# Two halves of 256 tokens: the second half's attention and routing placed between the row gathers of the first

## What is computed

```python
# attention: 8 MLA heads and 8 "fox" heads, causal, on h = modulate(rmsnorm(x)); x = x + gate * (o @ w_o)
# then, with h = modulate(rmsnorm(x)):
qp = (h @ w_pq).reshape(b, s, 8, 2, 128)
sc = einsum("bshpd,hpnd->bshpn", qp, sub_keys)           # 2 x 128 scores for each token and head
s1, i1 = top_k(sc[..., 0, :], 16); s2, i2 = top_k(sc[..., 1, :], 16)
top_s, top_c = top_k(s1[..., :, None] + s2[..., None, :], 16)
expert = i1[top_c // 16] * 128 + i2[top_c % 16]           # one of 16384
g = softmax(top_s)
a = einsum("bcd,bchkd->bchk", h, peer_u[expert])          # one row of 1024 floats for each choice
y = einsum("bchk,bchkd->bcd", g * gelu(a), peer_v[expert])
```

## Time and profile before

| | |
|---|---|
| profiled execution | 3415.21 us, span 3413.4 us |
| first block and final norm | 0 to 1295 us |
| attention of the second block, 512 tokens | 1295 to 1834 us |
| norm and routing up to the first gather | 1834 to 1891 us |
| gathers, dots and sums | 1891 to 3413 us |
| PE, DVE, ACT, POOL busy over the span | 80%, 56%, 29%, 48% |
| DMA | 666.49 MB; software queue (gathers) 41.6% of 16 engines' time, hardware queue 12.5% |

### The profile page before, as it was taken

The page is one execution under the profiler, slowest core; times in us unless marked ns, Lnnn a source line. Parts: engine busy times, 40 slices in busy tenths (PEclk is TensorE's granted clock), DMA queues, the critical chain, the costliest instruction groups (busy, mean ns, idle before and its releaser), DMA issues. The chain is left out here.

```text
span 3413.4 us, 37062 instructions
## 1 busy us (share of the span) xinstructions
PE 2742.4 (80%) x12788; PEld 1837.1 (54%) x12788; DVE 1909.3 (56%) x3608; ACT 1002.9 (29%) x1912; POOL 1623.8 (48%) x1464
## 2 busy tenths in 40 slices
PE   6997879999999697687988888777776777767777
PEld 6997878888889693244655333223222322222323
DVE  5366556666666754665443655555555555555552
ACT  2222155555555211322332122212212212222211
POOL 2443265555555230110001566666666666666665
PEclk8998989998989798888999999998988889989899
DMA  3333411111111341001102799999999999999998
GB/s 97 96 88 124 151 50 50 49 49 49 49 47 39 97 150 37 27 0 37 38 19 80 286 370 328 364 377 356 361 375 357 357 369 363 359 361 365 359 369 310
DMA packets 343486, 666.49 MB, mean 195 GB/s; under 512 B 22181, under 2 KB 209738, under 8 KB 343098
## 3 DMA queue, kind: packets, MB, share of 16 engines
q0 software_dynamic: 147456, 536.94, 41.6%
q1 hardware_dynamic: 194906, 127.75, 12.5%
q10 hardware_dynamic: 992, 0.13, 0.0%
HBM read 662.64 MB, written 2.10 MB: 195 GB/s over the span
## 5 line engine op out<-in xcount | busy, mean ns | idle before, releaser
L1867 PE MATMUL peer_py<-peer_vb,peer_diag 128*128 128x512 f32 x2048 | 1036.9, 655 | 353.1 <-issue 177.5
L1867 PEld LDWEIGHTS peer_py<-peer_vb,peer_diag 128*128 128x128 f32 x2048 | 405.5, 208 | 959.4 <-issue 767.9
L1716 DVE SCALAR_TENSOR_TENSOR peer_spare<-peer_ub,peer_hp 128x1024 bf16<-128x1024 f32 x512 | 623.5, 1218 | 475.9 <-DMA peer_ub<-in_peer_u,peer_idx 416.0
L1611 POOL DMA_INDIRECT peer_vb<-in_peer_v,peer_idx x512 | 480.3, 938 | 351.9 <-issue 140.9
L1603 POOL DMA_INDIRECT peer_ub<-in_peer_u,peer_idx x512 | 483.6, 945 | 169.7 <-issue 137.6
L1800 ACT ACTIVATE peer_diag<-keep_ident,peer_wt 128x128 f32<-128x128 f32 x512 | 190.8, 397 | 994.5 <-PE peer_py L1867 388.8
L862 PE MATMUL hgrn_pp<-p2n_hh,hgrn_wh 128*128 128x264 f32 x1024 | 226.4, 304 | 27.6 <-POOL hgrn_wl L733 27.6
L733 POOL TENSOR_TENSOR hgrn_wl<-p2n_w,hgrn_wh 128x1024 fp32r<-128x1024 f32 x64 | 153.9, 2405 | 180.4 <-ACT hgrn_wh L770 180.4
L862 PE MATMUL hgrn_pp<-p2n_hl,hgrn_wh 128*128 128x264 f32 x1024 | 218.1, 296 | 0.0
L862 PE MATMUL hgrn_pp<-p2n_hh,hgrn_wl 128*128 128x264 f32 x1024 | 216.7, 294 | 0.0
L862 PEld LDWEIGHTS hgrn_pp<-p2n_hh,hgrn_wh 128*128 128x128 f32 x1024 | 171.0, 203 | 28.9 <-POOL hgrn_wl L733 28.4
(11 more groups left out here) (369 smaller groups left out, 4762.7 us busy)
## 6 DMA issues: line engine op xcount, KB each, us to landing
p2n_w<-in_hgrn_w_in SPq DMA_DIRECT2D x64, 512.0 KB
p1n_w<-in_pool_w_in SPq DMA_DIRECT2D x32, 512.0 KB
pool_out_aw<-in_w_ada SPq DMA_DIRECT2D x16, 768.0 KB, 4.7
hgrn_out_aw<-in_w_ada SPq DMA_DIRECT2D x16, 768.0 KB, 4.9
pool_out_w<-in_pool_w_out SPq DMA_DIRECT2D x8, 1024.0 KB, 7.2
hgrn_out_w<-in_hgrn_w_out SPq DMA_DIRECT2D x8, 1024.0 KB, 6.7
p_w<-in_w_pq SPq DMA_DIRECT2D x8, 1024.0 KB
peer_ub<-in_peer_u,peer_idx POOLq DMA_INDIRECT x512
```

Source lines behind the costliest of these rows:

```text
L1611: pool.indirect_dma_start(out=vb[:, n % DEPTH, :], out_offset=None, in_=io["peer_v_2"], in_offset=bass.IndirectOffsetOnAxis(ap=idx[:, s, k ...
L1716: dve.scalar_tensor_tensor(out=spare[:, n % 2, :], in0=ub[:, n % DEPTH, :], scalar=1.0, in1=hp[:, t % 2, :], op0=ALU.mult, op1=ALU.mult, a ...
L1867: last = pe.matmul(py[:, h * 512:(h + 1) * 512], diag[:, n % DIAGS, :], vb[:, n % DEPTH, h * 512:(h + 1) * 512], start=n % (PH * TOPK) == ...
```

## The change

The second block is done for tokens 0 to 255 first, and then for tokens 256 to 511. All its phases take `half` and work on W = 256 columns. The keys and values of the first half are kept (`k_mla`, `k_fox`, `v_mla`, `v_fox`) for the second. `product_phase` is replaced for the attention's output by plain fp32 products (`attn_out_phase`). All weights of the second block are loaded twice.

`peer_phase` becomes a class `Peers` of 532 numbered ticks. At tick T GpSimd issues the u gather of step T + 6 and the v gather of step T - 15, VectorE does the dot of step T, ScalarE the diagonal and TensorE the sum of step T - 20. `beat(n)` runs n ticks at a place in another phase's lists, the same number on each of the four engines. 75 ticks lie in the routing of the first half (15 beats of 5), 8 in the norm, 21 in `latent_phase`, 60 in MLA, 60 in fox, 16 in the output product and 8 in the norm of the second half, 75 in its routing, and the last 209 in `finish_phase`. The h operand of the dot is copied from PSUM to `ht` in SBUF. `pr` of the heads has two banks in place of three, `pT_` one in place of two, and the fox weights of the second half one buffer.

```diff
+def norm_phase(nc, name, x, out, gain, tokens, shift=None, halves=None, ahead=None, beat=None):
...
+        def walk(entries, unit, name):
             for slot in range(U):
                 entries(0, slot)
+                beat(name)
             for g in range(N * U):
                 unit(g, lambda: entries(g // U + 1, g % U) if g // U + 1 < N else None)
+                beat(name)
...
+            slots = [[("raw", 0), ("raw", 2), ("raw", 1), ("raw", 3)],
+                     [("ones", r) for r in order] + [("v", 0), ("rot", 0)],
+                     [("rot", 2), ("rot", 1)], [("rot", 3)]]
...
+UNITS = TT * PH
+SLOTS = UNITS * TOPK
+U_BUFS, V_BUFS, DIAGS = 6, 6, 4
+U_LEAD, V_LAG, Y_LAG = 6, 15, 20
+TICKS = SLOTS + Y_LAG
+class Peers:
...
+        if tick + U_LEAD < SLOTS:
+            gather_u(tick + U_LEAD)
+        if 0 <= tick - V_LAG < SLOTS:
+            gather_v(tick - V_LAG)
...
+            dve.wait_ge(self.u_in[tick % U_BUFS], 16 * (tick // U_BUFS + 1))
+            if tick >= 2:
+                dve.wait_ge(self.dotted, tick - 1)
+            dve.scalar_tensor_tensor(out=self.spare[:, tick % 2, :], in0=self.ub[:, tick % U_BUFS, :], scalar=1.0,
+                                     in1=self.ht[:, t % HT, :], op0=ALU.mult, op1=ALU.mult,
+                                     accum_out=self.a[:, s, k:k + 1]).then_inc(self.dotted, 1)
...
+            pe.wait_ge(self.v_in[n % V_BUFS], 16 * (n // V_BUFS + 1))
+            pe.wait_ge(self.diag_done, n + 1)
...
         def _(pool):
+            for r in range(R):
                 pool.wait_ge(hit_in, r + 1)
                 which = bf[:, r % 2].rearrange("p j (a k) -> p j a k", k=1).to_broadcast([P, 2, TOPK, TOPK])
                 pool.tensor_tensor(hit[:, r % 2], hit[:, r % 2], which, ALU.mult).then_inc(hit_out, 1)
+                if r >= 1:
+                    peers.known = first + r
+                    beat("pool")
...
+            for r in range(R):
+                if r + 2 < PH:
+                    project(r + 2)
+                if r + 2 < R:
+                    scores(r + 2)
+                if r >= 1:
+                    beat("pe")
...
+            with Phase(nc, "hm0") as phh:
+                attention(0, phh.sb("hm", [P, KC, W]), lambda ticks: no_beat)
+            clear_semaphores(nc)
+            with Phase(nc, "peer") as ph4:
+                peers = Peers(nc, io, keep, ph4, out)
+                routing(0, peers, lambda ticks: no_beat)
+                peers.level()
+                attention(1, xT[:, :, 0:W], peers.beat)
+                peers.level()
+                routing(1, peers, peers.beat)
+                peers.level()
+                finish_phase(nc, peers)
```

More of the change, by code:

```diff
@@ L1399, in unit @@
                 values(g - 1)
-            walk(entries, unit)
+            walk(entries, unit, "pe")
             values(N * U - 1)
@@ new lines, in finish_phase, with _, load_queries @@
+def finish_phase(nc, peers):
+    with Phase(nc, "finish") as ph:
+        blk = ph.block()
+        @blk.tensor
+        def _(pe):
+            peers.run("pe", TICKS)
+        @blk.scalar
+        def _(act):
+            peers.run("act", TICKS)
+        @blk.vector
+        def _(dve):
+            peers.run("dve", TICKS)
+        @blk.gpsimd
+        def _(pool):
+            peers.run("pool", TICKS)
+def load_queries(io, sp, w, w_in, n):
+    view = io["w_pq_2"].rearrange("(k p) n -> p k n", p=P)
+    sp.dma_start(w[:, n % 2], view[:, :, n * 2 * P:(n + 1) * 2 * P]).then_inc(w_in[n % 2], 16)
@@ L1540, in peer_phase, with route_phase @@
+def route_phase(nc, io, keep, h2, w, w_in, peers, half, beat):
+    R = HT * PH
+    first = half * R
+    with Phase(nc, f"route{half}") as ph:
         skT = ph.sb("skT", [P, PH, 2, P])
-        qT = ph.sb("qT", [P, PH, 2, SEQ])
+        qT = ph.sb("qT", [P, PH, 2, W])
+        sc = ph.sb("sc", [P, 3, 2, NK])
         best = ph.sb("best", [P, 2, TOPK])
@@ L1582, in _ @@
                 sp.wait_ge(projected, 2 * (n - 1))
-                load(sp, n, n % 2)
-            for t in range(TT):
-                sp.wait_ge(y_taken, t + 1)
-                sp.dma_start(out[0, t * P:(t + 1) * P, :], rows[:, t % 2, :]).then_inc(stored[t % 2], 16)
-            for b in range(2):
-                sp.wait_ge(stored[b], 16 * TT // 2)
+                load_queries(io, sp, w, w_in, n)
         @blk.gpsimd
         def _(pool):
-            def chosen(r):
+            for r in range(R):
                 pool.wait_ge(hit_in, r + 1)
@@ L1807, in _ @@
+                if r >= 1:
+                    peers.known = first + r
+                    beat("pool")
+            peers.known = first + R
         @blk.tensor
@@ L1840, in scores @@
                 last.then_inc(scored, 1)
-            project(0, 0)
-            project(0, 1)
+            project(0)
             scores(0)
+            project(1)
+            scores(1)
             turn_h(0)
-            for n in range(1, 4):
-                project(n, 0)
-                project(n, 1)
-                scores(n)
-            for c in range(KC):
-                last = pe.matmul(py[:, c * P:(c + 1) * P], mod[:, 5 * KC + c:5 * KC + c + 1].to_broadcast([P, P]),
-                                 ident[:, :], start=True, stop=True)
@@ new lines, in routing, with route_ahead @@
+            def routing(half, peers, beat):
+                x = xT[:, :, half * W:(half + 1) * W]
+                with Phase(nc, f"p4{half}") as ph4:
+                    w = ph4.sb("w", [P, 2, KC, 2 * P])
+                    w_in = [ph4.sem("w_in0"), ph4.sem("w_in1")]
+                    def route_ahead(sp):
+                        for n in range(2):
+                            load_queries(io, sp, w, w_in, n)
+                    norm_phase(nc, f"mod2{half}", x, oT, col("norm2_g_2"), W,
+                               lambda c: mod[:, 3 * KC + c:3 * KC + c + 1], ahead=route_ahead, beat=beat(4))
+                    route_phase(nc, io, keep, oT, w, w_in, peers, half, peers.beat(5))
```

870 lines of the change are left out of this document (470 added, 400 removed).

## The result

The changed kernel takes 3510.8 us (median of 4 runs, 3499.1 to 3514.3) where the kernel before takes 3409.9 (4 runs, 3402.6 to 3417.6): ratio 1.0293, 95% interval 1.0266 to 1.032. It is 3% slower. I had forecast 3370, which would have been faster; 3511 lies at the upper edge of the stated range (3245 to 3515), on the side that I had given 0.29.

A forecast was written before the change was run, and what follows sets the result against it. Gather stage bound by DMA transfers, with 596 us ahead of it in which they could run. First gather 1636 + 245 + 647 + 268 + 581 = 3377 span, 3379 executed, lowered by 9 to 3370; own range 3300 to 3440, stated 3245 to 3515.

The forecast's parts named there:

- Part 1: Second block's first half alone, up to the first gather: 341 us in place of 596, first gather at 1636.
- Part 2: Price of one tick: DMA 2.88 us, POOL 2.97 including 0.49 for gathers held by dots reading two SBUF operands.
- A: Routing of half 0 with 75 ticks in 15 beats of 5: 245 us.
- B: Attention of half 1 with its norms, 173 ticks: 647 us, where pure transfer would be 498.
- Part 3: The woven stage from the first gather on: A 245, B 647, C 268, D 581 us.
- MLA: PE 9.6 a beat, POOL 10.1: Half 1's MLA in B, us per beat on each engine: 230 us with the start.
- R3: Rival, lockstep: each unit's chain is paid behind its ticks, B 800 us, total 3530; chance 0.13.
- C: Routing of half 1 with 75 ticks: 25 for its start plus 15 beats of 16.2, 268 us.
- Norm and latent: In B, half 1: 29 ticks, 84 us for DMA plus 9 for weights plus tail, 98 us.
- the last norm with the start of C: Norm 27 us; C's start 25, with rows under way covering some 12 of PE's projections and turns.
- Late weights: Sign that the forecast would be wrong: the weights' loads waiting behind the gathers.
- D: Last 209 ticks, 387 gathers at 1.45 us plus 20 for the tail: 581 us.

The follow-up runs named there:

- run 14: Changed kernel with u gather lead 3 for 6 in most of B, first weights loaded a block earlier, dot reading h from PSUM in A, C, D: 3413.6 us, ratio 1.0039.
- run 18: Kernel of run 15 again, on a 3305 chip: 3320.1 us.
- Run 4: Changed kernel with two ticks in place of three beside every unit of MLA and fox, 3305 chip: 3474.9 us.
- run 9: Changed kernel with u lead 3 and v lag 17 only beside norm, latent, MLA and output product of half 1, 3305 chip: 3396.8 us.
- run 10: Changed kernel with the attention's squares moved from POOL to ScalarE and its cosine products to DVE, 3305 chip: 3419.6 us.
- run 1: Changed kernel with half 1's attention and norms run without ticks, B's 173 ticks in a stage of their own, 3305 chip: 3523.8 us.
- run 13: Kernel of run 9 with half 1's first weights of MLA, fox and output product loaded one block earlier, 3405 chip: 3421.8 us.
- run 16: Kernel of run 15 with PE also leaving out half of the y product in B's ticks, 3405 chip: 3393.5 us.
- run 3: Changed kernel with MLA's first rotation product moved one slot later on PE and DVE, 3305 chip: 3461.4 us.
- run 15: Kernel of run 9 with the dot replaced by a sum of the u row (one SBUF operand), 3405 chip: 3455.6 us.

## Why the prediction was wrong

**Part 1, right.** First gather 1636.05 for 1636, though with luck in it: the second block began at 1292 in place of 1295, and the terms partly cancel: norm 10.5 (12), latent 41.5 (38), MLA 116 (105), fox 89 (88), output product 33 (35), norm 10.5 (13), routing 43.5 (45). MLA's reciprocals did halve; its chain did not.

**Part 2, right in kind, too high.** Gathers are held as the stores of the earlier trace rows showed: 299 of 1024 took over 1 us, up to 2.97, 186.5 us in all or 0.36 per tick where I took 0.49. The dot in A (1640 to 1880), as a group by line, in the changed kernel and in run 14, where it reads PSUM:

```profile
L1746 DVE SCALAR_TENSOR_TENSOR peer_spare<-peer_ub,peer_ht 128x1024 bf16<-128x1024 f32 x75 | 97.0, 1334 | 20.5 <-DMA peer_ub<-in_peer_u,peer_idx 20.0 <-issue 0.2
```

```profile
L1808 DVE SCALAR_TENSOR_TENSOR peer_spare<-peer_ub,route_pT 128x1024 bf16<-128x1024 f32 x75 | 87.3, 1217 | 10.3 <-DMA peer_ub<-in_peer_u,peer_idx 10.3
```

Its mean is 0.12 us longer, but the gathers don't do that. 63 of the 75 dots take their 1.21 to 1.23 us, and 12 take 1.64 to 2.12. Those 12 are the ones that run into POOL's `chosen`, once in each of 12 beats:

```profile
1659.06 1.95 POOL L1874 TENSOR_TENSOR route_hit<-route_hit,route_bf 128x512 bf16<-128x512 bf16 x1 [5.88 <-DVE route_hit L2035]
1660.03 2.06 DVE L1746 SCALAR_TENSOR_TENSOR peer_spare<-peer_ub,peer_ht 128x1024 bf16<-128x1024 f32 x1
1661.16 1.78 POOL L1714 DMA_INDIRECT peer_ub<-in_peer_u,peer_idx  x1 [0.15 <-issue]
```

In the whole changed kernel 437 dots overlap gathers and no other work of POOL; they take 1.22 us on average, and none over 1.3. Of 39 that overlap a tensor operation of POOL 23 take longer, and `chosen` itself takes up to 1.96 in place of 1.06. So "they show no hold on DVE" was right of gathers, and the forecast had no term for POOL's tensor operations. The Trainium skill, "SBUF — State Buffer", section "Who interferes with whom", has a DVE instruction with two SBUF inputs contend with a GpSimd instruction that reads SBUF. For `chosen` the trace agrees in both directions; for gathers it shows the hold in one direction only. In B the holds decided little: with them gone, on top of lead 3, B is 10 us shorter (run 18).

**Part 3, B, wrong; this is the step that failed.** "MLA: PE 9.6 a beat, POOL 10.1" took for each beat the largest sum of an engine. That is a bound from below, and I used it as the time. Measured were 13.6 us a beat in MLA (271 us in 20), with PE at 10.0 and POOL at 8.1 busy. The engines are tied tick by tick: the u gather of tick k needs the dot of tick k (6 buffers less a lead of 6 is no slack), and the v gather of tick k PE's product of tick k - 1. So POOL can't begin its 7.4 us of issues until DVE has worked through the unit's norms and rotations, and the next unit's squares and cosines stand behind these issues. Run 4 shows the tick at POOL's price behind the chain, run 9 the 68 us that come back with slack on POOL's side, run 10 the same wait from the other end. I had the mechanism as R3, gave it 0.13, and priced it at 800 for B (825 with the 25 of C's start) and 3530 in all; measured were 776 with C's start and 3511. Its nearness in the total is partly luck: in fox, by run 1, ticks and chain are not simply added. What I held against it, "scores run two units ahead", is true and beside the point, since the loop seen in the waits doesn't go through the scores. "All four engines may be only 6 ticks apart" was wrong on the side that mattered: POOL may be behind DVE by 6 and ahead by none.

**Norm and latent, and the last norm with the start of C, too low by 28 and 17.** The rows under way were to cover the stretches without ticks ("cover some 12 of it"). POOL stood 47 us at the start of C (run 14), where I had let the rows under way cover 12. Late weights, which I had named as what would make it wrong, are worth 14 us (run 13).

**C's beats, too low by 17.** I took 16.2 for each. Between successive fifth u gathers they take 15.5 to 16.7, but 18.0 to 20.8 in the five in which PE has a projection of 7.1 us ahead of five ticks of products, and 22.4 in the last; my sum had left these projections to the cover at C's start. **D and the transfers, right**: 577 for 581, at 362 GB/s and 0.96 of the engines.

**What I did not price at all** is the split's own cost. I summed region B as ticks and never wrote down that the two halves in series take 720 us where 596 had stood. With that line the change's gain is what the ticks hide, less 125, and the question is put to the hiding from the start.

What stays open is the rest of B. With the lead right it takes 697 to 711 us, where I had 672 with the start of C. None of PE (12 us, for 149 taken off), the holds (10 for 72) and the weights (14 for 43) is its bound alone. PE and holds taken away together left 679 on a 3405 chip (run 16). The order of the lists fits that, but no run here changed this order with all else kept, so it isn't shown.

## What to carry to other kernels

Where work is woven by hand into several in-order lists, the largest engine sum is a bound and not a time: write down for each list which entry of another list it may not pass, with the number of buffers less the lead as the slack, and give every engine some slack on both sides. Price a split first with nothing woven in (both halves in series); only what that leaves can be won. And a long wait in the table need not be a cause: run 3 took 28 of the 33.9 us off the wait that it was aimed at, 19.8 came up in another, and MLA stayed; an edit to another engine's distance took 45 us off MLA and halved this wait with it.

## What the runs showed of the hardware

Two kinds of chips. On those of the 3405 kind the gather stage has stops in which several engines and the transfers stand. One of them, POOL of the kernel before in order of time:

```profile
3001.16 0.94 POOL L1603 DMA_INDIRECT peer_ub<-in_peer_u,peer_idx  x1 [0.30 <-issue]
3006.33 0.94 POOL L1611 DMA_INDIRECT peer_vb<-in_peer_v,peer_idx  x1 [4.22 <-remote]
```

The transfers from 2980 to 3020 us, in steps of one, first for the kernel before on a 3405 chip, then for run 9 on a 3305 chip:

```profile
GB/s 299 274 291 336 397 389 426 406 418 422 418 422 418 422 422 406 422 422 422 414 418 422 426 422 414 414 156 25 147 377 233 356 340 303 348 352 365 377 393 418
```

```profile
GB/s 422 418 406 393 426 414 393 406 422 418 397 401 426 406 393 406 422 414 397 406 418 422 393 410 418 418 393 410 418 418 393 410 418 418 397 401 422 418 397 401
```

Both run at some 410 GB/s; one has a hole of 3 us and a slow climb after it. Counted in steps of 1 us over 460 us of D, the rate is below 200 GB/s in 29 steps in the kernel before, 7 in the changed one, 15 in run 13 and 17 in run 14, and in none in runs 3 and 9. So the 362 to 364 GB/s from which I worked out 2.88 us per tick are the mean of a faster rate, such holes and the slow stretches behind them; on the other kind a pair of gathers takes 2.54 us (run 18, D), close to POOL's 2.48. There POOL and its holds are the bound of D, and the PSUM operand is worth 20 us. Where the holes are, taking the holds away brought no time in A and C of run 14, and run 15 has MLA at 244 against 215 for the same kernel in run 18. What the stops are, and why A and C don't gain there, the traces don't show.

Waits without a named releaser don't measure these stops. The traces of the 3405 chips have many ("issue" above all: PE 184 us in the kernel before from 1891 to 3390, 32 in the changed one, 111 in run 14), those of the 3305 chips next to none. But the same wait of DVE for the reciprocal's input in MLA stands in the changed kernel without a releaser and in run 3 with one:

```profile
DVE mla_rs L1563 <- issue: 35.2, 4, 14.0
```

```profile
DVE mla_rs L1563 <- ACT mla_rs L1515: 36.1, 4, 14.9
```

Three of the four waits have the same length to 0.01 us in both (5.85, 7.74, 7.64), and in both DVE starts 0.03 us behind ScalarE's write. Nothing stopped there; the trace lacks the releaser. A stop is sure only where the transfers show it too.
